# The order of four PSUM banks in the first slot of a feed-forward loop chunk

## The chip, the cores and the metric

The kernel runs on one core of a Trainium2 chip. The metric is the device time of one execution in microseconds (us), as the median of several runs; lower is better. The engines are called as the profile calls them: PE is TensorE (PEld its weight loads), DVE VectorE, ACT ScalarE, POOL GpSimd, and SP issues the weight transfers.

## What is computed

A stack of two transformer layers (an mLSTM mixer in the first, a differential attention in the second) with four feed-forward layers, two gated per-layer embeddings and a shared key-value projection, and behind it one hybrid block of convolution and dilated attention. 256 tokens, model width 1024, everything in float32. The change touches the four feed-forward layers alone, which are

```python
D_MODEL = 1024; SEQ = 256; D_FF = 2816

def rms_norm(x, g):
    xf = x.astype(jnp.float32)
    y = xf * lax.rsqrt(jnp.mean(xf * xf, axis=-1, keepdims=True) + EPS)
    return (y * g.astype(jnp.float32)).astype(x.dtype)

def swiglu(x, w_in, w_out):
    gate, up = jnp.split(x @ w_in, 2, axis=-1)
    return (jax.nn.silu(gate) * up) @ w_out
...
        h = swiglu(rms_norm(x, g[0]), w_ffn_in[layer, 0], w_ffn_out[layer, 0])
        x = x + 0.5 * rms_norm(h, g[1])
```

and the same again with g[4] and g[5], in both layers of the stack.

## The kernel before

**Weights come in slots.** All weights stream through one sequence of 226 slots of 128 x 2048 elements. SP loads a slot into one of three raw buffers, ACT rounds it to the format of the fast product (w_hi, L623), POOL subtracts to get the rest (w_lo, L590), and PE uses both. w_hi and w_lo have six buffers each. The activations are split in the same way (xT_hi, xT_lo), and a product is made of three: high by high, low weights by high activations, high weights by low activations.

**A feed-forward layer** has 11 chunks of 256 hidden columns. A chunk needs two slots for gate and up (four of the eight row blocks of the model width in each, "half" 0 and 1) and one slot for the down projection, which adds into the four acc banks. The layers are F0, F1, F2 and F3. Chunks 0, 1 and 10 are written out; chunks 2 to 9 are in a loop of four turns with two chunks in each (L2158), so there are 32 loop chunks in the whole kernel. The order in the loop is: gate and up of chunk n, down projection of chunk n-1, gate and up of chunk n+1, and so on.

**In a loop chunk** (`gate_up_rows`, L2052) the hidden columns are the rows of the result, so the weights are the stationary operand. Per row block k, per part (gate, up) and per half of the columns j there is a `high` product (L2067): w_hi against xT, whose 512 columns are the high and the low activations of 256 tokens, and a `low` product (L2073): w_lo against the 256 columns of xT_hi, added into the first half of the same bank. That is 16 high and 16 low products in a slot. Gate goes to the banks gu[:, 0] and tb[:, 1], up to gu[:, 1] and tb[:, 0]. A bank is opened by the high product of k = 0 of the first slot and closed in the second.

**What the banks wait for.** The gate banks of the chunk before must have been read (the wait for h_ready), and the up banks too: DVE multiplies up by the activated gate in place (L1326), ACT copies its high half out (L801) and DVE subtracts the low half (L1330), which counts ht_lo_ready. In the first loop chunk of a layer (n = 2) the hidden values of chunk 1 come by another way: PE turns them with four transposes into tb[:, 0] right ahead of the chunk (L2108), ACT copies the high half (L731, L767), and DVE subtracts the low half in one instruction (L1358 in F0 and F2, L1384 in F1 and F3), which counts ht_lo_ready.

**After a slot** the last products count tile0_used and slot_used, by which ACT knows that a buffer of w_hi may be written again; the last gate products of the second slot count gate_in_psum, on which DVE starts to scale the gate (L1312 to L1315).

Of the kernel before, what the change touches and what calls it, by code (L numbers as in the profile page):

```python
# [31 lines left out]
P = 128  # L32
# [5 lines left out]
NIT = FF // CH  # L38
# [98 lines left out]
def program(nc, A, out):  # L137
    ctx = ExitStack()
    with ctx:
        def sb(name, shape, dt=F32):  # L140
            return ctx.enter_context(nc.sbuf_tensor(name, shape, dt))

        def sem(name):
            return ctx.enter_context(nc.semaphore(name))
# [3 lines left out]
        w_hi = sb("w_hi", [P, NSPL, SLOT], F32R)  # L148
        w_lo = sb("w_lo", [P, NSPL, SLOT], F32R)
        xT = sb("xT", [P, KT, 2, TILES * P], F32R)  # L150
        xT_hi, xT_lo = xT[:, :, 0, :], xT[:, :, 1, :]
# [76 lines left out]
        at = 1024  # L228
# [48 lines left out]
        tile0_used = sem("tile0_used")  # L277
        slot_used = sem("slot_used")
# [11 lines left out]
        h_ready = sem("h_ready")  # L290
        ht_in_psum = sem("ht_in_psum")
        ht_hi_ready = sem("ht_hi_ready")
        ht_lo_ready = sem("ht_lo_ready")
        rs_row_in_psum = sem("rs_row_in_psum")
        rs_row_ready = sem("rs_row_ready")
        gate_in_psum = sem("gate_in_psum")
# [58 lines left out]
        def ht_count(f, n, t=0):  # L355

            return (NIT + 1) * f + n + 1 + t
# [1572 lines left out]
        def _(pe):  # L1930
            mm = nc.tensor.matmul
# [117 lines left out]
            def ffn(name, following):  # L2049
                f, s0 = FFN_NO[name], S[name]  # L2050

                def gate_up_rows(n, i, a):  # L2052

                    for half in range(2):
                        slot = a.plus(half)
                        pe.wait_ge(lo_ready, slot.count())
                        for part, pair_of in enumerate((gate_rows, up_rows)):
                            if half == 0 and part == 0:  # L2060
                                pe.wait_ge(h_ready, i * 4 + (2 * NIT * f + 2 * n))
                            if half == 0 and part == 1:
                                pe.wait_ge(ht_lo_ready, i * 2 + ht_count(f, n - 1))

                            def high(k, j):
                                at = 512 * k + 256 * part + P * j
                                return mm(pair_of(j), w_hi[:, slot.spl, at:at + P],  # L2067
                                          xT[:, 4 * half + k, :, :].rearrange("p a c -> p (a c)"),
                                          start=(half == 0 and k == 0), stop=(half == 1 and k == 3))

                            def low(k, j):
                                at = 512 * k + 256 * part + P * j
                                return mm(pair_of(j)[:, 0:2 * P], w_lo[:, slot.spl, at:at + P],  # L2073
                                          xT_hi[:, 4 * half + k, :], start=False, stop=False)

                            for k in range(4):
                                for product in ((high, low), (low, high))[half == 1 and k == 3]:
                                    done = [product(k, j) for j in range(2)]
                            for j in range(2):
                                if part == 1:  # L2080
                                    done[j].then_inc((tile0_used, slot_used)[j], 1)
                                elif half == 1:
                                    done[j].then_inc(gate_in_psum, 1)

                def down_n(n, turn, slot):

# [71 lines left out]
                with pe.Fori(0, (NIT - 3) // 2) as i:  # L2158
                    for d in (0, 1):
                        gate_up_rows(2 + d, i, At(s0 + 5 + 3 * d, i))  # L2160
                        down_n(1 + d, i, At(s0 + 7 + 3 * d, i))


                n, a = NIT - 1, At(s0 + FFN_SLOTS - 4)
# [514 lines left out]
```

## Time and profile before

| | |
|---|---|
| median of three runs | 1376.75 us (1374.72 to 1377.45) |
| the profiled execution | 1375.41 us, its span 1373.4 us |
| granted clock of PE, mean | 0.999 |
| PE busy | 1357.0 us, 99% of the span |
| POOL busy | 1134.7 us, 83% |
| ACT and DVE busy | 662.9 us and 606.5 us |
| loop chunks | 32, in four groups that start at 43.3, 339.2, 602.2 and 860.0 us |

Times in the rows below are microseconds from the start of the span. A row of the timeline has the start, the time that it covers, the engine and line, the operation with its output and inputs, how many instructions were merged into the row (x), and in square brackets the idle time of the engine just before it with what ended that. Matmuls overlap: one of 512 columns shows 0.39 us, but the next starts earlier than that, so the distance from start to start is what a product costs.

### The profile page before, as it was taken

How to read it: one execution, taken by the hardware profiler on the slowest of the kernel's cores; microseconds unless marked ns; L12 is line 12 of the kernel's file. 1: busy time of each engine (PE TensorE's matmuls, PEld its weight loads, DVE VectorE, ACT ScalarE, POOL GpSimd, SP SyncE). 2: the span in 40 equal slices, each digit the busy share in tenths (PEclk: the TensorE clock that was granted, in tenths of full speed). 3: DMA queues.
4: the chain of work that ended last, by engine and by line, in shares of the span. 5: the costliest groups of instructions: out<-in, count | busy, mean ns of one | idle time of the engine just before them, and what ended most of it. 6: DMA issues, size and time to landing. Idle time of an engine off the chain costs nothing.

```text
span 1373.4 us, 19730 instructions
## 1 busy us (share of the span) xinstructions
PE 1357.0 (99%) x6803; PEld 1127.9 (82%) x6803; DVE 606.5 (44%) x1554; ACT 662.9 (48%) x773; POOL 1134.7 (83%) x913
## 2 busy tenths in 40 slices
PE   8999999999999999999999999999999999999997
PEld 5888888888888888888888778888888888888886
DVE  6233344654333356323333885333356135762224
ACT  5444444556444455544443675444446444554531
POOL 5999977849999967999998549999968987679882
PEclk9999999999999999999999999999999999999999
DMA  8666654627655545666555426655545554346550
GB/s 271 214 204 205 203 184 142 203 85 230 203 194 184 192 160 180 214 191 207 183 183 186 138 81 206 214 187 183 185 163 189 186 182 154 128 153 240 184 170 31
DMA packets 160960, 246.98 MB, mean 180 GB/s; under 512 B 8924, under 2 KB 99844, under 8 KB 160772
## 3 DMA queue, kind: packets, MB, share of 16 engines
q1 hardware_dynamic: 158612, 239.42, 53.3%
q10 hardware_dynamic: 2288, 6.75, 1.3%
q8 instruction: 38, 0.62, 0.2%
q14 instruction: 22, 0.18, 0.0%
HBM read 245.10 MB, written 1.05 MB: 179 GB/s over the span
## 4 chain that ended last, share of the span: by engine, by line
POOL 59%; PE 21%; issue 17%; DMA 1%; ACT 0%; DVE 0%; POOLq 0%; SPq 0%; ACTq 0%; DVEq 0%
POOL w_lo L590 59%; PE acc L1981 5%; PE acc L1984 5%; PE acc L1982 5%; DMA w_raw<-in_w_ffn_in 1%; PE tb L1984 1%; PE tb L1982 1%; PE gu L1982 1%; PE tb L1981 1%; PE gu L1984 1%; PE gu L1981 1%; PE tb L2552 1%; PE gu L2517 0%; PE tb L2526 0%; DMA x_res<-in_x 0%
## 5 line engine op out<-in xcount | busy, mean ns | idle before, releaser
L590 POOL TENSOR_TENSOR w_lo<-w_raw,w_hi 128x512 fp32r<-128x512 f32 x896 | 1129.7, 1305 | 211.7 <-ACT w_hi L623 209.2
L623 ACT CAST w_hi<-w_raw 128x2048 fp32r<-128x2048 f32 x225 | 427.6, 1909 | 135.9 <-DMA w_raw<-in_w_ffn_in 37.0
L2067 PE MATMUL gu<-xT,w_hi 128*128 128x512 f32 x512 | 202.4, 395 | 0.0
L2067 PE MATMUL tb<-xT,w_hi 128*128 128x512 f32 x512 | 202.2, 395 | 0.0
L1981 PE MATMUL acc<-w_hi,xT 128*128 128x512 f32 x496 | 198.2, 400 | 0.0
L1982 PE MATMUL acc<-w_lo,xT 128*128 128x512 f32 x496 | 193.2, 389 | 0.0
L1984 PE MATMUL acc<-w_hi,xT 128*128 128x512 f32 x468 | 182.7, 390 | 0.0
L1312 DVE TENSOR_TENSOR arena<-gu,arena 128x256 f32<-128x256 f32 x64 | 27.2, 424 | 300.5 <-PE gu L2067 300.5
L2073 PE MATMUL tb<-xT,w_lo 128*128 128x256 f32 x512 | 140.3, 280 | 0.0
L2073 PE MATMUL gu<-xT,w_lo 128*128 128x256 f32 x512 | 139.8, 279 | 0.0
L1981 PE MATMUL gu<-w_hi,xT 128*128 128x512 f32 x312 | 123.7, 396 | 2.2 <-ACT xT L655 2.0
L1982 PE MATMUL gu<-w_lo,xT 128*128 128x512 f32 x312 | 121.5, 389 | 0.0
L2073 PEld LDWEIGHTS tb<-xT,w_lo 128*128 128x128 f32 x512 | 96.4, 188 | 20.2
L2073 PEld LDWEIGHTS gu<-xT,w_lo 128*128 128x128 f32 x512 | 96.2, 188 | 19.1
L1982 PEld LDWEIGHTS acc<-w_lo,xT 128*128 128x128 f32 x496 | 93.3, 188 | 18.2 <-issue 0.2
L1981 PEld LDWEIGHTS acc<-w_hi,xT 128*128 128x128 f32 x496 | 93.3, 188 | 18.3 <-issue 0.6
L1984 PEld LDWEIGHTS acc<-w_hi,xT 128*128 128x128 f32 x468 | 87.8, 188 | 18.8
L797 ACT ACTIVATE arena<-gu 128x256 f32<-128x256 f32 x32 | 12.3, 383 | 184.4 <-DVE gu L1315 184.3
L2067 PEld LDWEIGHTS tb<-xT,w_hi 128*128 128x128 f32 x512 | 97.1, 190 | 2.6
L2067 PEld LDWEIGHTS gu<-xT,w_hi 128*128 128x128 f32 x512 | 96.3, 188 | 2.5
L1984 PE MATMUL gu<-w_hi,xT 128*128 128x512 f32 x192 | 74.9, 390 | 0.0
L1981 PEld LDWEIGHTS gu<-w_hi,xT 128*128 128x128 f32 x312 | 58.6, 188 | 14.5 <-issue 2.5
(373 smaller groups left out, 2057.4 us busy)
## 6 DMA issues: line engine op xcount, KB each, us to landing
w_raw<-in_w_ffn_in SPq DMA_DIRECT2D x176, 512.0 KB, 4.6
w_raw<-in_w_ffn_out SPq DMA_DIRECT2D x88, 512.0 KB, 4.2
w_raw<-in_w_in SPq DMA_DIRECT2D x80, 512.0 KB, 4.5
w_raw<-in_mlstm_w_in SPq DMA_DIRECT2D x24, 512.0 KB, 4.3
w_raw<-in_w_ple_gate SPq DMA_DIRECT2D x16, 512.0 KB, 4.3
w_raw<-in_w_kv SPq DMA_DIRECT2D x16, 512.0 KB, 4.3
w_raw<-in_mlstm_w_out SPq DMA_DIRECT2D x8, 512.0 KB, 4.5
w_raw<-in_diff_w_q SPq DMA_DIRECT2D x8, 512.0 KB, 4.1
```

The source lines that it names most:

```text
L590: ins = pool.tensor_tensor(w_lo[:, slot.spl, cols], w_raw[:, slot.raw, cols], w_hi[:, slot.spl, cols].bitcast(F32), ALU.subtract)
L623: nc.scalar.copy(w_hi[:, slot.spl, :], w_raw[:, slot.raw, :]).then_inc(hi_ready, 1)
L797: nc.scalar.activation(sg[:, j, :], gate_rows(j)[:, 0:2 * P], ACT.Silu).then_inc(silu_ready, 1)
L1312: v.tensor_tensor(part, low, rs_row, ALU.mult).then_inc(row_step, 1)
L1981: mm(out, xh, wh, start=(half == 0 and k == 0), stop=False)
L1982: mm(out, xh, wl, start=False, stop=False)
L1984: last = mm(out, xl, wh, start=False, stop=(half == 1 and k == 3))
L2067: return mm(pair_of(j), w_hi[:, slot.spl, at:at + P], xT[:, 4 * half + k, :, :].rearrange("p a c -> p (a c)"), start=(half == 0 and k == 0 ...
L2073: return mm(pair_of(j)[:, 0:2 * P], w_lo[:, slot.spl, at:at + P], xT_hi[:, 4 * half + k, :], start=False, stop=False)
L2552: ins = nc.tensor.transpose(tb[:, 1, tok(k)], h_s[:, H_PLACE[c], t, tok(k)], ident[:])
```

## The change

In the first slot of a loop chunk the two loops over part and over k change places. Before, all 16 gate products ran through k = 0 to 3, high j = 0, 1 then low j = 0, 1, and then the 16 up products likewise. Now each k has four high products (gate, gate, up, up) and then four low ones in the same order of banks. The wait for ht_lo_ready, which stood ahead of the up products, stands now ahead of the first up product of k = 0, that is behind the second product of the slot. The slot's counts stay on its last two products. The second slot keeps its order.

```diff
--- before.py
+++ after.py
@@ -2056,31 +2056,35 @@
                     for half in range(2):
                         slot = a.plus(half)
                         pe.wait_ge(lo_ready, slot.count())
-                        for part, pair_of in enumerate((gate_rows, up_rows)):
-                            if half == 0 and part == 0:
-                                pe.wait_ge(h_ready, i * 4 + (2 * NIT * f + 2 * n))
-                            if half == 0 and part == 1:
-                                pe.wait_ge(ht_lo_ready, i * 2 + ht_count(f, n - 1))
-
-                            def high(k, j):
-                                at = 512 * k + 256 * part + P * j
-                                return mm(pair_of(j), w_hi[:, slot.spl, at:at + P],
-                                          xT[:, 4 * half + k, :, :].rearrange("p a c -> p (a c)"),
-                                          start=(half == 0 and k == 0), stop=(half == 1 and k == 3))
-
-                            def low(k, j):
-                                at = 512 * k + 256 * part + P * j
-                                return mm(pair_of(j)[:, 0:2 * P], w_lo[:, slot.spl, at:at + P],
-                                          xT_hi[:, 4 * half + k, :], start=False, stop=False)
-
+
+                        def high(k, part, j):
+                            at = 512 * k + 256 * part + P * j
+                            return mm((gate_rows, up_rows)[part](j), w_hi[:, slot.spl, at:at + P],
+                                      xT[:, 4 * half + k, :, :].rearrange("p a c -> p (a c)"),
+                                      start=(half == 0 and k == 0), stop=(half == 1 and k == 3))
+
+                        def low(k, part, j):
+                            at = 512 * k + 256 * part + P * j
+                            return mm((gate_rows, up_rows)[part](j)[:, 0:2 * P], w_lo[:, slot.spl, at:at + P],
+                                      xT_hi[:, 4 * half + k, :], start=False, stop=False)
+
+                        if half == 0:
+                            pe.wait_ge(h_ready, i * 4 + (2 * NIT * f + 2 * n))
                             for k in range(4):
-                                for product in ((high, low), (low, high))[half == 1 and k == 3]:
-                                    done = [product(k, j) for j in range(2)]
+                                for product in (high, low):
+                                    for part in range(2):
+                                        if k == 0 and part == 1 and product is high:
+                                            pe.wait_ge(ht_lo_ready, i * 2 + ht_count(f, n - 1))
+                                        done = [product(k, part, j) for j in range(2)]
                             for j in range(2):
-                                if part == 1:
-                                    done[j].then_inc((tile0_used, slot_used)[j], 1)
-                                elif half == 1:
-                                    done[j].then_inc(gate_in_psum, 1)
+                                done[j].then_inc((tile0_used, slot_used)[j], 1)
+                            continue
+                        for part in range(2):
+                            for k in range(4):
+                                for product in ((high, low), (low, high))[k == 3]:
+                                    done = [product(k, part, j) for j in range(2)]
+                            for j in range(2):
+                                done[j].then_inc((tile0_used, slot_used)[j] if part else gate_in_psum, 1)
 
                 def down_n(n, turn, slot):
 
```

## Rows read from the trace of the kernel before

**Rows 1.** The page: the span, busy times, and the granted clock in 40 slices.

```profile
span 1373.4 us, 19730 instructions
PE 1357.0 (99%) x6803; PEld 1127.9 (82%) x6803; DVE 606.5 (44%) x1554; ACT 662.9 (48%) x773; POOL 1134.7 (83%) x913
PEclk9999999999999999999999999999999999999999
```

**Rows 2.** Waits of PE over the span: us in total, times, longest.

```profile
PE gu L1981 <- ACT xT L655: 2.0, 1, 2.0
...
PE gu L1981 <- POOL w_lo L590: 0.2, 1, 0.2
```

**Rows 3.** The page's groups of instructions: high products of the loops on gu.

```profile
L2067 PE MATMUL gu<-xT,w_hi 128*128 128x512 f32 x512 | 202.4, 395 | 0.0
```

**Rows 4.** Timeline of PE: first and twelfth of twelve products on one bank.

```profile
303.64 0.39 PE L1981 MATMUL acc<-w_hi,xT 128*128 128x512 f32 x1
...
306.14 0.39 PE L1984 MATMUL acc<-w_hi,xT 128*128 128x512 f32 x1
```

**Rows 5.** Timeline of PE: a down projection, 24 products, and the chunk behind it.

```profile
54.58 0.62 PE L2016 MATMUL acc<-w_hi,hT_hi 128*128 128x512 f32 x2
...
60.03 0.39 PE L2067 MATMUL gu<-xT,w_hi 128*128 128x512 f32 x1
```

**Rows 6.** Timeline of PE, steady chunk: gate k=0 and k=2, up, second slot, down, next.

```profile
126.66 0.39 PE L2067 MATMUL gu<-xT,w_hi 128*128 128x512 f32 x1
...
128.04 0.40 PE L2067 MATMUL gu<-xT,w_hi 128*128 128x512 f32 x1
...
129.43 0.40 PE L2067 MATMUL gu<-xT,w_hi 128*128 128x512 f32 x1
...
132.22 0.40 PE L2067 MATMUL gu<-xT,w_hi 128*128 128x512 f32 x1
...
137.82 0.62 PE L2016 MATMUL acc<-w_hi,hE_hi 128*128 128x512 f32 x2
...
143.28 0.39 PE L2067 MATMUL gu<-xT,w_hi 128*128 128x512 f32 x1
```

**Rows 7.** Timeline, first loop chunk of F0: products one and three, DVE's low half.

```profile
43.34 0.48 PE L2067 MATMUL gu<-xT,w_hi 128*128 128x512 f32 x1
...
43.89 0.28 PE L2073 MATMUL gu<-xT,w_lo 128*128 128x256 f32 x1
...
44.24 0.69 DVE L1358 TENSOR_TENSOR hT_lo<-tb,hT_hi 128x512 fp32r<-128x512 f32 x1 [1.88 <-ACT hT_hi L731]
```

**Rows 8.** Timeline: third chunk of F0, its low half, and that of the sixth.

```profile
76.80 0.39 PE L2067 MATMUL gu<-xT,w_hi 128*128 128x512 f32 x1
...
77.35 0.41 DVE L1330 TENSOR_TENSOR hT_lo<-tb,hT_hi 128x256 fp32r<-128x256 f32 x1
...
125.08 0.42 DVE L1330 TENSOR_TENSOR hE_lo<-tb,hE_hi 128x256 fp32r<-128x256 f32 x1
```

**Rows 9.** Timeline, first loop chunk of F1: first product, DVE's low half.

```profile
339.16 0.48 PE L2067 MATMUL gu<-xT,w_hi 128*128 128x512 f32 x1
...
340.06 0.69 DVE L1384 TENSOR_TENSOR hT_lo<-tb,hT_hi 128x512 fp32r<-128x512 f32 x1 [5.34 <-ACT hT_hi L767]
```

**Rows 10.** Timeline, second loop chunk of F0: ACT, DVE, products 17 and 18.

```profile
59.83 1.91 ACT L623 CAST w_hi<-w_raw 128x2048 fp32r<-128x2048 f32 x1 [2.80 <-DMA w_raw<-in_w_ffn_in]
...
62.38 0.41 DVE L1330 TENSOR_TENSOR hE_lo<-tb,hE_hi 128x256 fp32r<-128x256 f32 x1
...
62.84 0.50 PE L2067 MATMUL gu<-xT,w_hi 128*128 128x512 f32 x1
63.18 0.39 PE L2067 MATMUL tb<-xT,w_hi 128*128 128x512 f32 x1
```

**Rows 11.** Timeline: POOL's back-to-back stretch in F0; ACT ahead of the third chunk.

```profile
46.66 30.10 POOL L590 TENSOR_TENSOR w_lo<-w_raw,w_hi 128x512 fp32r<-128x512 f32 x24
...
74.80 1.91 ACT L623 CAST w_hi<-w_raw 128x2048 fp32r<-128x2048 f32 x1 [2.87 <-DMA w_raw<-in_w_ffn_in]
```

## Prediction

> **What bounds the kernel now.** I read the page's busy times first, then the waits of TensorE, then the rows of the two loop chunks in order of time. TensorE (PE) is busy for 99% of the span, GpSimd (POOL) for 83% [rows 1]. The chain that ended last runs mostly through POOL, so I looked at what PE really waited for: in the whole span the matmul line L1981 waited 2.0 us once for ScalarE and 0.2 us once for POOL, and no wait of PE is longer [rows 2]. PE never runs short of split weights; it is the bound, and the chain is drawn through POOL only because POOL works back to back in the same time. What adds time to PE's stream therefore adds it to the span, unless a later wait of PE shrinks by the same amount, and there is hardly a later wait that could.
>
> The edit touches the first of the two slots of each gate-and-up chunk. There are 32 such chunks: eight in each of four feed-forward layers. A slot is 16 products of 512 columns ("high") and 16 of 256 columns ("low"), so the loops hold 512 high products on gu and on tb each [rows 3], and half of them lie in first slots.
>
> **Part 1, what is removed or added: nothing.** The same 32 products, with the same operands, lengths and weight loads, stand in a first slot before and after. The increments of the slot stay on its last two products, and the second slot is the same. DMAs, POOL's, ACT's and DVE's instructions stay as they are. Only two things move: the order of banks, and the wait for ht_lo_ready.
>
> **Part 2, the order of banks (spacing of products).** First, does it matter to a product which bank the one before it wrote? Eleven products in a row on one bank of acc go from 303.64 to 306.14, 2.50 / 11 = 0.227 us each [rows 4]. In the down projections two banks alternate, and 24 products take from 54.58 to 60.03, 5.45 / 24 = 0.227 us each [rows 5]. So one bank or two is the same to 0.001 us, and I expect no more from four.
>
> What does cost is the mix of lengths. At 0.227 us for 512 columns and half of that, 0.1135 us, for 256, a slot would take 16 x 0.3405 = 5.45 us. A chunk in the steady state takes 132.22 - 126.66 = 5.56 us for the first slot and 137.82 - 132.22 = 5.60 us for the second [rows 6]. So 0.11 us of a first slot is excess. If four banks removed it all, the gain would be 0.11 x 32 = 3.5 us, or 4.0 us with the rounding of the rows against me (0.125 us a chunk): the bound of a gain.
>
> The other bound comes from the second slot. It has two places at which four low products stand in a row (the low ones of k=2, then k=3 begins with its own low ones), one in the gate part, with four high ones behind it, and one in the up part; the first slot has no such place. It takes 0.04 us more, and the first slot has a cheap first group: its first two k-steps take 1.38 us, the next two 1.39 and the four of the up part 2.79 [rows 6]. Set aside the cheap entrance of 0.01 us, and two runs of four lows cost 0.03 us of the 0.04: about 0.015 us each, 0.02 at most. The changed first slot has four runs of "four high, four low" in place of eight of "two, two". The first keeps its cheap entrance from the down products; the three others cost 0.015 us each: 0.045 us a chunk, x 32 = 1.4 us slower. Bounds of this term: 4.0 us faster and 0.02 x 4 x 32 = 2.6 us slower. I take +1.4, since the rows with a run of four lows are of the very products that are moved.
>
> The Trainium skill (Perfetto Trace Analysis, section Matmul Optimizations) says that all eight PSUM banks should be put to use so that more can go on at once. By that rule the four banks would be worth something, up to the 4.0 us above; by the rows of one bank and of two they are worth nothing.
>
> **Part 3, the wait for ht_lo_ready moves up by 14 products.** Now PE passes it behind 16 gate products, some 2.78 us into the chunk; after the change behind two, 0.45 us into it (0.54 us where a transpose stands ahead: 43.89 - 43.34 [rows 7]). Behind the wait stands all of PE's stream, and behind that the gate and up results for which DVE and ACT wait. What matters is when VectorE has written the last of the low halves of h, which is what the semaphore counts.
>
> In the steady state it is in time. Before the chunk that starts at 126.66 the last subtraction ends at 125.08 + 0.42 = 125.50 [rows 8], 1.16 us ahead of the start. Twenty-five of the 32 chunks repeat these rows to 0.01 us, and one has its low half 0.45 us ahead; they cost nothing, and the cover has 1.16 + 0.45 = 1.6 us left. The wait for h_ready stays at the chunk's start; it counts an earlier step of the same chain on DVE and was never seen to bind.
>
> It is late in the first chunk of each layer. There the low half is made from transposes that PE issues just ahead of the chunk, then a copy on ACT, then one subtraction on DVE. In layer F0 the chunk starts at 43.34, the third product at 43.89, and DVE ends at 44.24 + 0.69 = 44.93 [rows 7]. In F1 the chunk starts at 339.16 and DVE ends at 340.06 + 0.69 = 340.75 [rows 9]: 1.59 us into the chunk in both, and the other two layers repeat it. What PE needs to restart I read at the one place where this very wait already binds, in the second chunk of F0: DVE ends at 62.38 + 0.41 = 62.79, and the product behind the wait starts at 62.84, 0.05 us later; its successor follows after 0.34 us in place of 0.23, so another 0.10 us goes into filling up again [rows 10]. The stall of a first chunk is then 1.59 + 0.05 - 0.54 + 0.10 = 1.20 us, and four of them are 4.8 us.
>
> The second chunk of F0 is the fifth place. It starts at 60.03 [rows 5] and the low half is ready at 62.79; it now loses 0.14 us (0.04 ahead of the product at 62.84 and 0.10 behind it). Its time is not set by PE: ACT's copies of h stand behind a 1.91 us weight cast at 59.83 that waited for a DMA, while POOL subtracts back to back from 46.66 to 76.76 [rows 10, 11]. So it stays at 62.79 when PE comes later. PE comes 1.20 us later, reaches its third product at 60.03 + 1.20 + 0.45 = 61.68, and starts it at 62.84: 1.16 + 0.10 = 1.26 us of stall, less the 0.14 that goes, +1.12 us net. The third chunk of F0 starts at 76.80 now and at 79.1 then [rows 8]; its low half is ready at 77.35 + 0.41 = 77.76 [rows 8], again behind a cast that waited for a DMA [rows 11], so it is in time by then. Sum of part 3: 4.80 + 1.12 = 5.9 us. Its bounds are narrow, 5.5 us without the refill of 0.10 in four of the five places, and 6.6 us if the low half of F0's third chunk moved with PE, so that this chunk had to wait too (77.76 + 0.05 - 77.25 + 0.10 = 0.66).
>
> The skill has a rule that speaks against this change (Perfetto Trace Analysis, section Matmuls): groups should rotate through banks so that the emptying of one overlaps with the products of the next. Taking all four banks at once gives that overlap up for a slot: the up banks used to be emptied under 16 gate products.
>
> **How the numbers follow.** +5.9 (stalls) + 1.4 (spacing) = +7.3 us on the profiled run. That run took 1375.41 us, of which 1373.4 are its span; the median of the three runs is 1376.75, 1.3 us above it, and I add the sum to the median: 1376.75 + 7.3 = 1384.1 us, +0.53%. About 0.2% (2.75 us) is what a measurement of this kernel can tell from no change.
>
> **Rivals.** (a) *Rotation pays.* The excess of the mixed slots is the reuse of a bank two products later, and goes: 1376.75 + 5.9 - 4.0 = 1378.7 us, within 0.2%. Against it: one bank in a row shows no such cost. Chance 6%. (b) *The stalls are given back.* PE's stalls sit in five places, and with PE later, POOL and the DMAs are further ahead, so later waits shrink. That would leave 1.4 us or so: 1378 us. Against it: PE's listed waits of 2.0 and 0.2 us are at 14 us or too small to give back 5.9. Chance 4%. (c) *Faster.* If four banks in turn let the array take one column in every cycle of the granted 2.4 GHz (the granted clock is 0.9 or more in every slice [rows 1]), a first slot would take 16 x (512 + 256) / 2.4 = 5.12 us, an estimate, in place of 5.56: 0.44 x 32 = 14.1 us won, 1376.75 + 5.9 - 14.1 = 1368.6 us. It decides from 5.9 / 32 = 0.18 us won per chunk. For it speaks that 0.227 us is more than 512 / 2.4 = 0.213; against it that one bank and two give the same 0.227, so the rest isn't a matter of banks. Chance 3%. On this the skill (TensorE: Matmul & The Clock Gate, section Back-to-back issue gap) gives 512 columns 215.7 ns when nothing else binds; by that the slot would be 5.2 us, close to (c), but the trace shows 0.227 us throughout. (d) *The change stalls steadily*: if the wait were late in every chunk, not in five, 32 x 1.2 = 38 us, 1415 us. The rows at 125.50 exclude it by 1.6 us; 1%. The forecast has 86%.
>
> Range: spacing from 0 to +2.6 and stalls from 5.5 to 6.6 give 1382.3 to 1386.0; the median of runs can sit 1 us to either side; reaching a little towards (a), where part of the excess goes, the range is 1380.8 to 1386.8. Chances: slower by over 0.2% 0.87 (the forecast and (d)), within 0.2% 0.10 ((a) and (b)), faster 0.03 ((c)).
>
> **What would show it.** In the changed trace: in the first chunk of each layer a gap of about 1.2 us behind the second product, ended by the DVE subtraction L1358 or L1384; in the second chunk of F0 one of 1.26 us ended by L1330 at about 62.8; no gap in the others. The period of a steady loop chunk with its down projection, now 143.28 - 126.66 = 16.62 us [rows 6], should be 16.64 to 16.68. If it is 16.50 or less, rival (a) or (c) holds and the spacing term is wrong in sign. If the first-chunk gaps are there but the span is not longer, (b) holds.

## The result, and the profile after

| | before | after |
|---|---|---|
| median of the runs | 1376.75 us (5 runs) | 1382.63 us (5 runs, 1381.60 to 1384.39) |
| ratio | | 1.0051, 95% interval 1.0040 to 1.0061 |
| span of the profiled execution | 1373.4 us | 1379.7 us |
| granted clock of PE, mean | 0.999 | 0.999 |

The kernel became slower, by 5.9 us in the medians and by 6.3 us in the two profiled spans. The quotient of the two medians is 1.0043; it lies inside the interval of the recorded ratio, which in microseconds reaches from 5.5 to 8.4. So the total alone fixes the size of the change only to about 3 us, and the steps below are read from the traces. The page of the changed kernel shows the same count of instructions as [rows 1] and hardly another busy time. The groups of instructions show where the wait went: the high products on gu (L2062, formerly L2067, [rows 3]) now have idle time ahead of them.

```profile
span 1379.7 us, 19730 instructions
PE 1359.2 (99%) x6803; PEld 1128.9 (82%) x6803; DVE 608.1 (44%) x1554; ACT 662.8 (48%) x773; POOL 1134.3 (82%) x913
...
L2062 PE MATMUL gu<-xT,w_hi 128*128 128x512 f32 x512 | 202.6, 396 | 5.2 <-DVE hT_lo L1384 1.9
```

The waits of PE, in us in total, times and longest, answer [rows 2]. Three lines are new, and they are the five places that the prediction named: two first chunks with L1384 (F1, F3), two with L1358 (F0, F2), and one chunk with L1330.

```profile
PE gu L2062 <- DVE hT_lo L1384: 1.9, 2, 0.9
PE gu L2062 <- DVE hT_lo L1358: 1.8, 2, 0.9
PE gu L1981 <- ACT xT L655: 1.7, 1, 1.7
PE gu L2062 <- DVE hE_lo L1330: 1.5, 1, 1.5
```

The timeline of the first loop chunk of F1, against [rows 9]: two products go, then nothing until DVE's subtraction ends at 342.74 + 0.69 = 343.43, and the third starts at 343.49. The wait view calls that 0.94 us, because it takes a matmul of 0.40 us as busy to its end; from start to start it is 343.49 - 342.15 = 1.34 us where 0.23 would do, and about 0.1 us more is lost behind the third (its successor starts 0.33 us later, not 0.23).

```profile
341.84 0.48 PE L2062 MATMUL gu<-xT,w_hi 128*128 128x512 f32 x1
342.15 0.40 PE L2062 MATMUL tb<-xT,w_hi 128*128 128x512 f32 x1
...
342.74 0.69 DVE L1384 TENSOR_TENSOR hT_lo<-tb,hT_hi 128x512 fp32r<-128x512 f32 x1 [5.34 <-ACT hT_hi L767]
...
343.49 0.50 PE L2062 MATMUL gu<-xT,w_hi 128*128 128x512 f32 x1 [0.94 <-DVE hT_lo L1384]
```

The second loop chunk of F0, against [rows 10]. The third product starts at 63.15, 1.68 us after the 61.47 at which it would have followed. ACT's cast, which began at 59.83 in the kernel before, begins here at 60.14, when its DMA has landed; the copies behind it and the subtraction are later by as much.

```profile
60.14 1.91 ACT L623 CAST w_hi<-w_raw 128x2048 fp32r<-128x2048 f32 x1 [2.55 <-DMA w_raw<-in_w_ffn_in]
...
61.01 0.39 PE L2062 MATMUL gu<-xT,w_hi 128*128 128x512 f32 x1
61.24 0.39 PE L2062 MATMUL tb<-xT,w_hi 128*128 128x512 f32 x1
...
62.68 0.41 DVE L1330 TENSOR_TENSOR hE_lo<-tb,hE_hi 128x256 fp32r<-128x256 f32 x1
...
63.15 0.50 PE L2062 MATMUL gu<-xT,w_hi 128*128 128x512 f32 x1 [1.52 <-DVE hE_lo L1330]
63.49 0.39 PE L2062 MATMUL tb<-xT,w_hi 128*128 128x512 f32 x1
```

A steady chunk, against [rows 6]: first slot from 129.31 to 134.90, second to 140.49, next chunk at 145.94. The low half of the chunk before (127.73 + 0.42 = 128.15) is 1.16 us ahead of the start, as in [rows 8].

```profile
127.73 0.42 DVE L1330 TENSOR_TENSOR hE_lo<-tb,hE_hi 128x256 fp32r<-128x256 f32 x1
...
129.31 0.39 PE L2062 MATMUL gu<-xT,w_hi 128*128 128x512 f32 x1
...
134.90 0.40 PE L2062 MATMUL gu<-xT,w_hi 128*128 128x512 f32 x1
...
140.49 0.39 PE L2016 MATMUL acc<-w_hi,hE_hi 128*128 128x512 f32 x1
...
145.94 0.39 PE L2062 MATMUL gu<-xT,w_hi 128*128 128x512 f32 x1
```

The two slots take 5.59 and 5.59 us where they took 5.56 and 5.60: the first lost 0.024 us and the second, whose order was not touched, won 0.017. Over six steady chunks of F1 (second to eighth) the difference can be read without rounding trouble: 455.61 - 355.89 = 99.72 us before and 459.52 - 359.76 = 99.76 after, that is 0.007 us a chunk and 0.2 us in all 32. First the two rows of the kernel before, then those of the changed one:

```profile
355.89 0.39 PE L2067 MATMUL gu<-xT,w_hi 128*128 128x512 f32 x1
...
455.61 0.39 PE L2067 MATMUL gu<-xT,w_hi 128*128 128x512 f32 x1
```

```profile
359.76 0.39 PE L2062 MATMUL gu<-xT,w_hi 128*128 128x512 f32 x1
...
459.52 0.39 PE L2062 MATMUL gu<-xT,w_hi 128*128 128x512 f32 x1
```

For all kernels below, the table has the stretch from the first product of a layer's first loop chunk to that of its eighth, in us, taken from the starts in the traces. It leaves out everything ahead of the loops, which differs from run to run (last section).

| kernel | F0 | F1 | F2 | F3 | sum |
|---|---|---|---|---|---|
| before | 116.55 | 116.45 | 116.43 | 116.43 | 465.86 |
| after | 119.43 | 117.69 | 117.66 | 117.66 | 472.44 |
| e1_wait_only | 118.42 | 117.62 | 117.62 | 117.61 | 471.27 |
| e2_early_turn | 116.41 | 116.39 | 116.39 | 116.39 | 465.58 |
| e3_runs_of_four | 116.45 | 116.51 | 116.45 | 116.45 | 465.86 |
| e4_four_banks_by_twos | 116.34 | 116.34 | 116.34 | 116.34 | 465.36 |
| e5_wait_behind_eight | 118.19 | 116.67 | 116.68 | 116.71 | 468.25 |
| e9_early_turn_f1_f3 | 118.93 | 116.39 | 116.39 | 116.39 | 468.10 |
| e10_copies_before_cast | 117.69 | 116.39 | 116.39 | 116.39 | 466.86 |
| e11_wait_at_front | 118.31 | 116.45 | 116.42 | 116.47 | 467.65 |
| e12_old_order_both_fixes | 116.41 | 116.34 | 116.34 | 116.34 | 465.43 |

The change added 6.6 us to the loops and 6.3 us to the span. Of the 0.3 us between them, 0.2 lie ahead of F0's loop, where nothing was changed yet (it starts at 43.13 and not at 43.34); the stretches between the loops and behind the last are shorter by 0.1 us in all.

### The profile page after: what moved, and what is told of

Same layout as the page of the kernel before. It is cut to its first block, busy times and chain, and to the rows that moved or that the text cites. A ratio compares the mean times of both kernels' runs of the same rounds, so it can differ in the third digit from the quotient of the medians.

```text
span 1379.7 us, 19730 instructions
## 1 busy us (share of the span) xinstructions
PE 1359.2 (99%) x6803; PEld 1128.9 (82%) x6803; DVE 608.1 (44%) x1554; ACT 662.8 (48%) x773; POOL 1134.3 (82%) x913
## 3 DMA queue, kind: packets, MB, share of 16 engines
HBM read 245.10 MB, written 1.05 MB: 178 GB/s over the span
## 4 chain that ended last, share of the span: by engine, by line
POOL 58%; PE 21%; issue 18%; DMA 1%; DVE 1%; ACT 1%; POOLq 0%; SPq 0%; ACTq 0%; DVEq 0%
POOL w_lo L590 58%; PE acc L1981 5%; PE acc L1984 5%; PE acc L1982 5%; PE tb L1984 1%; PE tb L1981 1%; PE tb L1982 1%; PE gu L1981 1%; PE gu L1982 1%; PE gu L1984 1%; PE tb L2556 1%; PE gu L2521 0%; PE tb L2530 0%; DMA w_raw<-in_w_ffn_in 0%; ACT w_hi L623 0%
## 5 line engine op out<-in xcount | busy, mean ns | idle before, releaser
L2062 PE MATMUL gu<-xT,w_hi 128*128 128x512 f32 x512 | 202.6, 396 | 5.2 <-DVE hT_lo L1384 1.9
L2062 PE MATMUL tb<-xT,w_hi 128*128 128x512 f32 x512 | 201.6, 394 | 0.0
L2068 PE MATMUL tb<-xT,w_lo 128*128 128x256 f32 x512 | 135.2, 280 | 0.0
L2068 PE MATMUL gu<-xT,w_lo 128*128 128x256 f32 x512 | 134.5, 280 | 0.0
L2062 PEld LDWEIGHTS gu<-xT,w_hi 128*128 128x128 f32 x512 | 96.5, 188 | 15.2 <-DVE hT_lo L1384 2.7
L2062 PEld LDWEIGHTS tb<-xT,w_hi 128*128 128x128 f32 x512 | 96.9, 189 | 7.9
```

What stands on the lines that cost most here:

```text
L2062: return mm((gate_rows, up_rows)[part](j), w_hi[:, slot.spl, at:at + P], xT[:, 4 * half + k, :, :].rearrange("p a c -> p (a c)"), start=(h ...
L2068: return mm((gate_rows, up_rows)[part](j)[:, 0:2 * P], w_lo[:, slot.spl, at:at + P], xT_hi[:, 4 * half + k, :], start=False, stop=False)
```

## The experiments

The theory is that the wait, moved up by 14 products, makes nearly all of the loss. The rival is that the order of four banks costs something by itself, in each chunk.

### The wait alone, and the order alone

e1 keeps the old order and moves only the wait:

```diff
-                            if half == 0 and part == 1:
-                                pe.wait_ge(ht_lo_ready, i * 2 + ht_count(f, n - 1))
...
                                     done = [product(k, j) for j in range(2)]
+                                    if half == 0 and part == 0 and k == 0 and product is high:
+                                        pe.wait_ge(ht_lo_ready, i * 2 + ht_count(f, n - 1))
```

> The kernel before with one edit: the wait for ht_lo_ready stands behind the first two gate products, the order of products is the old one. Theory (the moved wait carries the change): gaps of about 1.2 us behind the second product in the first loop chunk of each layer and one of 1.5 to 2.0 us in the second chunk of F0, none elsewhere; steady period 16.62 us as before; span +6.0 to +6.6 us, as long as that of the changed kernel to within 0.5 us. Rival (the order of the banks is what costs): no more than 1 us slower than before.

Measured: 1381.88 us, ratio to before 1.0042 (1.0028 to 1.0056), where the whole change had 1.0051 (1.0040 to 1.0061). (The profiled execution was 7.0 us longer in its span than that of the kernel before; 1.5 of these lie ahead of F0's loop, as the last section tells.) The loops of F1 to F3 are 1.17 to 1.19 us longer than before, the changed kernel's 1.23 to 1.24. The waits are the same ones:

```profile
PE gu L2070 <- DVE hT_lo L1358: 1.9, 2, 0.9
PE gu L2070 <- DVE hT_lo L1384: 1.9, 2, 0.9
```

The gap in F0's second chunk was 0.81 us, not the 1.5 to 2.0 expected; more on that below. In three layers the wait alone gives the change's loss to 0.07 us, most of which is the 0.007 us a chunk. The rival is out as a large cost.

e3 has the other half: two banks and the old wait, but runs of four high and four low products in the first slot.

```diff
-                            for k in range(4):
+                            if half == 0:
+                                for k2 in (0, 2):
+                                    for product in (high, low):
+                                        for k in (k2, k2 + 1):
+                                            done = [product(k, j) for j in range(2)]
+                            for k in range(4) if half else ():
```

> The kernel before with one edit: in each half of the first slot (gate, then up, two banks each) the products run four high, four low, as in the changed kernel, and the wait stays behind 16 gate products. If the mix of lengths causes the 7 ns by which a steady chunk grew (11.168 to 11.175 us): period 16.627 us, no gaps, span +0.2 us. If four banks cause it: period 16.620 us.

e4 turns it round: four banks, but lengths by twos, on top of e2 (below).

```diff
                             for k in range(4):
-                                for product in (high, low):
-                                    for part in range(2):
+                                for part in range(2):
...
+                                    for product in (high, low):
```

> As the early-turn kernel, but each k of the first slot runs gate high, gate low, up high, up low (two and two), so the four banks are taken in turns of two and the lengths alternate as before the change. If lengths cause the 7 ns: period 16.620 us; if the banks do: 16.627 us. The wait stands behind four products in place of two, so the gap in F0's second chunk is 0.2 us shorter than in the early-turn kernel.

The timeline of PE in F1, from the second to the eighth chunk, first for e3 and then for e4:

```profile
357.64 0.39 PE L2067 MATMUL gu<-xT,w_hi 128*128 128x512 f32 x1
...
457.40 0.39 PE L2067 MATMUL gu<-xT,w_hi 128*128 128x512 f32 x1
```

```profile
359.07 0.39 PE L2062 MATMUL gu<-xT,w_hi 128*128 128x512 f32 x1
...
458.79 0.39 PE L2062 MATMUL gu<-xT,w_hi 128*128 128x512 f32 x1
```

99.76 us with two banks and runs of four, as in the changed kernel; 99.72 us with four banks and runs of two, as before. So the 0.007 us a chunk belong to the order of lengths, and taking four banks in place of two costs and wins nothing. The starts within one steady chunk say the same: from product to product e3 and the changed kernel agree to about 1 ns, and so do e4 and the kernel before. F0's second chunk had no gap at all in e4 (its loop is 116.34 us), so what was expected of that gap could not be read. Each ran once, in 1377.36 and 1378.76 us. e3's span of 1375.3 us is 1.9 us over the kernel before, and 1.8 of these lie ahead of F0's loop, not in the loops; e4's loop in F0 begins 3.4 us late, in part for the reason given at e2.

### Taking away what makes the wait late

In a first chunk the low half is late because PE turns chunk 1's hidden values right ahead of the loop. e2 turns them one tile of a down projection earlier, in all four layers; so that nothing is overwritten, chunk 0's halves go to hE.

```diff
-                    hi, lo = h_rows(n) if n else (hT_hi, hT_lo)
+                    hi, lo = h_rows(n)
                     for t in range(TILES):
                         down_tile(slot, hi, lo, t, n == 0, False)
+                        if t == 0 and between:
+                            between()
...
-                down_n(0, None, At(s0 + 4))
-                turn_h(1, hs_next if name in SKEWED else hs)
+                down_n(0, None, At(s0 + 4), lambda: turn_h(1, hs_next if name in SKEWED else hs))
```

and L731, L767, L1358 and L1384 write h_rows(n) in place of hT.

> The changed kernel with the cause of the first-chunk waits taken away: chunk 0's hidden halves go to the other pair of buffers (hE), and the transposes of chunk 1's hidden values stand between the two tiles of the down projection ahead of the loop, 2.7 us earlier. Theory: the four first-chunk gaps of 1.2 us are gone (4.8 us), the gap in the second chunk of F0 stays and grows to about 2.4 us since PE comes 1.2 us earlier to it while its low half is ready at the same time; span 1375.9 to 1376.5 us, 3.3 to 3.8 us under the changed kernel. Rival (order of banks): still about 6 us over the kernel before.

Measured: 1379.15 us, 1.0020 (1.0011 to 1.0029) of before. All four first-chunk gaps are gone, and each loop takes 116.4 us. But the total is 3.3 us over before and not 2.5 to 3.1, and it is made of something else: the gap in F0's second chunk, expected to grow to 2.4 us, was not there, and a new loss appeared ahead of F0's loop, which began at 48.42 in place of 43.34. By then the low half of the second chunk was in time (ready at 63.91, the chunk at 65.07). Ahead of F0's loop DVE has chunk 1's hidden values too late for the earlier transposes, PE waits 1.92 us, and the products behind run at about half speed, 0.99 us for two in place of 0.45. The granted clock was 0.50 (the lower level, 1.2 GHz) from 44 to 47 us. In e4 PE waited 1.59 us at the same place and the granted clock stayed at 1.00; what decides between the two is not shown. The profiled execution of e2 was the slowest of its kernel (1380.45 us), so its other executions need not have this stretch. First the timeline of PE, then the view by windows (the stretch, busy PE, PEld, DVE, ACT and POOL with their counts, granted clock, DMA share, GB/s):

```profile
43.56 0.99 PE L2114 MATMUL tb<-ident,arena 128*128 128x128 f32 x4 [1.92 <-DVE arena L1339]
44.21 1.20 PE L2016 MATMUL acc<-w_hi,hE_hi 128*128 128x512 f32 x2
45.20 1.05 PE L2019 MATMUL acc<-w_lo,hE_hi 128*128 128x512 f32 x2
```

```profile
44.00:45.00 1.00, 1.00 (x5) 0.90 (x4) 0.00 (x0) 0.41 (x1) 1.00 (x2) 0.50 0.41 143
```

So e9 leaves F0 as it was:

```diff
+                down_n(0, None, At(s0 + 4),
+                       None if name == "F0" else lambda: turn_h(1, hs_next if name in SKEWED else hs))
+                if name == "F0":
+                    turn_h(1)
```

> The changed kernel with the transposes of chunk 1's hidden values between the two tiles of the down projection, and chunk 0's hidden halves in hE, in F1, F2 and F3 only; F0 keeps its place for them. Theory: the loops of F1, F2 and F3 take 116.4 us each in place of 117.7 (3.8 us in all), F0's loop stays at 118.4 to 119.4; 3.5 to 3.8 us under the changed kernel, 2.2 to 3.2 over the kernel before; and F0's prelude, which the early turn lengthened by some 3 us, is back. Rival (the early turn costs elsewhere what it saves): the stretches between the loops grow by 1 us each.

Measured: 1378.21 us, 1.0018 (1.0009 to 1.0027). That is 2.4 us over the kernel before, where 2.2 to 3.2 were expected, and 4.4 us under the changed kernel, more than the 3.5 to 3.8 expected: F0's loop too was 0.5 us shorter, by a smaller gap in its second chunk. The loops of F1, F2 and F3 take 116.39 us, and the stretches between them are 0.01 to 0.14 us longer, not 1 us. In F1 the subtraction now ends at 339.33 + 0.69 = 340.02, 1.24 us ahead of the chunk:

```profile
339.33 0.69 DVE L1384 TENSOR_TENSOR hT_lo<-tb,hT_hi 128x512 fp32r<-128x512 f32 x1 [2.62 <-ACT hT_hi L767]
...
341.26 0.39 PE L2062 MATMUL gu<-xT,w_hi 128*128 128x512 f32 x1
341.49 0.39 PE L2062 MATMUL tb<-xT,w_hi 128*128 128x512 f32 x1
341.72 0.39 PE L2062 MATMUL gu<-xT,w_hi 128*128 128x512 f32 x1
```

### The size of the stall

If a stall is (low half) minus (time of the products ahead of the wait), it can be dosed. e5 puts eight products ahead of the wait, e11 none.

```diff
-                            for k in range(4):
-                                for product in (high, low):
-                                    for part in range(2):
-                                        if k == 0 and part == 1 and product is high:
...
+                            for k2 in (0, 2):
+                                for part in range(2):
+                                    if k2 == 0 and part == 1:
+                                        pe.wait_ge(ht_lo_ready, i * 2 + ht_count(f, n - 1))
+                                    for k in (k2, k2 + 1):
+                                        for product in (high, low):
```

> The changed kernel with blocks of two k: eight gate products, then eight up products, twice, so that the wait for ht_lo_ready stands behind eight products (1.48 us into a first chunk) in place of two. Theory (stall = time from the chunk's start to the low half, 1.59 + 0.05, less the time of the products ahead of the wait, + 0.10 to fill up): 0.26 us in each first chunk, so F1, F2 and F3 loops are 116.7 us each (116.4 without a stall, 117.7 in the changed kernel), and the whole is within 2 us of the kernel before. Rival (a cost per chunk of opening all four banks early, whenever the wait is met): loops as long as in the changed kernel.

Measured: 1378.16 us, 1.0016 (1.0006 to 1.0025), 2.4 us over before, a little outside the 2 us. F1 to F3 take 116.67, 116.68 and 116.71 us: 0.22 to 0.28 us over before where 0.26 was worked out. F0's second chunk stalled 1.5 us all the same (1.4 more than in the kernel before), and that is the rest. e11 is the kernel before with the wait moved to the front:

```diff
                                 pe.wait_ge(h_ready, i * 4 + (2 * NIT * f + 2 * n))
-                            if half == 0 and part == 1:
                                 pe.wait_ge(ht_lo_ready, i * 2 + ht_count(f, n - 1))
```

> The kernel before, order of products untouched, with the wait for ht_lo_ready ahead of the first product of the chunk. Theory: the first-chunk stall is 1.59 + 0.05 and what it takes to fill up, so 1.65 to 1.8 us in place of 1.2; the loops of F1, F2 and F3 take 118.0 to 118.3 us each; F0's second chunk stalls 0.45 us more than with the wait behind two products. Steady chunks still none (cover 1.16 us): period 16.620 us.

Measured in one execution: 1384.24 us. The view of waits, below, has each first-chunk wait 0.5 us longer than in the changed kernel, and in the timeline behind it the first product of F1's loop starts 0.06 us after DVE ends (343.75 + 0.69 = 344.44):

```profile
PE gu L2065 <- DVE hT_lo L1384: 2.8, 2, 1.4
PE gu L2065 <- DVE hT_lo L1358: 2.8, 2, 1.4
```

```profile
343.75 0.69 DVE L1384 TENSOR_TENSOR hT_lo<-tb,hT_hi 128x512 fp32r<-128x512 f32 x1 [5.34 <-ACT hT_hi L767]
...
344.50 0.50 PE L2065 MATMUL gu<-xT,w_hi 128*128 128x512 f32 x1 [1.40 <-DVE hT_lo L1384]
```

The expectation put these stalls into the loops; standing ahead of the first product, they lie in the stretch before it, which grew from 179.27 to 180.91 us ahead of F1, by 1.64 us, and by 1.56 and 1.66 us ahead of F2 and F3. That is 1.59 + 0.05 with nothing to fill up again, because the product behind the transposes pays that anyway. So the stalls are 1.6, 1.2 and 0.26 us behind 0, 2 and 8 products, as worked out from the one row each. What was expected of F0's second chunk, 0.45 us more than with the wait behind two products, did not come: it stalled 1.8 us, as in the changed kernel.

### F0's second chunk

e10 is e9 with ScalarE's two copies of h ahead of its third weight cast in each loop chunk:

```diff
-                    ahead(a.plus(2))
                     for j in range(2):
                         act.wait_ge(h_ready, i * 4 + (2 * NIT * f + 2 * n + j + 1))
                         nc.scalar.copy(h_rows(n)[0][:, j, :], up_rows(j)[:, 0:2 * P]).then_inc(row_hi_ready, 1)
+                    ahead(a.plus(2))
```

> As the early turn in F1 to F3, and in every loop chunk ScalarE copies the high halves of h out of the up banks before its third weight cast, not behind it. Theory (F0's second chunk waits because the copies stand behind a cast that waits for its DMA): the gap in F0's second chunk goes, F0's loop is 116.4 + 1.2 = 117.6 us, the other three 116.4; 0.5 to 1.9 us under the run with the early turn alone, about 1.2 us over the kernel before. Rival (the late low half in F0 comes from DVE or PE): the gap stays.

Measured: 1377.52 us, 1.0011 (1.0002 to 1.0021), 0.7 us under e9. F0's loop takes 117.69 us, 1.3 more than the others by its first chunk; the second has no gap. The copy of the second bank is made at 60.76, as soon as DVE has written it, and the cast follows:

```profile
60.76 0.38 ACT L800 CAST hE_hi<-tb 128x256 fp32r<-128x256 f32 x1 [1.31 <-DVE tb L1326]
61.03 1.92 ACT L623 CAST w_hi<-w_raw 128x2048 fp32r<-128x2048 f32 x1
...
61.17 0.42 DVE L1330 TENSOR_TENSOR hE_lo<-tb,hE_hi 128x256 fp32r<-128x256 f32 x1
...
62.74 0.39 PE L2062 MATMUL gu<-xT,w_hi 128*128 128x512 f32 x1
```

The low half is ready at 61.59, 1.15 us ahead of the chunk, as in the steady state. So it was the place behind the cast that made this one late. That this execution began its loop late is not the reason: e1's began at the same 44.8 and had the gap. In the kernels with the old place the low half was ready 1.05 us after the end of the cast (in e2 1.35), and the cast began when its DMA had landed, at 59.83 in the kernel before, 60.14 in the changed one and 59.46 in e9.

Last, e12 has both edits on the kernel before, with its order and wait untouched:

> The kernel before, order of products and place of the wait untouched, with the two edits that took waits away: the early turn in F1 to F3 and ScalarE's copies ahead of its third cast. If it could beat the kernel before, it would be by what waits there still cost: 0.09 us at each of three loop entries (a transpose stands no longer just ahead) and 0.14 us in F0's second chunk. Loops of 116.34 us in F1 to F3 (116.43 to 116.45 before) and 116.4 in F0 (116.55), 0.1 us back in each stretch ahead of a loop: no difference that can be measured, within 0.1% of before.

Measured: 1376.0 us, 1.0004 (0.9995 to 1.0013), and loops shorter by 0.43 us in all. Its total cannot be told from the kernel before, so no kernel here is shown to beat that. In F0's second chunk the low half is now ready at 60.04, 2.75 us earlier than before, which is e10's finding once more.

## Why the prediction was right

The forecast was 1384.1 us in a range of 1380.8 to 1386.8; measured were 1382.63. The mechanism held: five stalls at the moved wait, in the five chunks named. Two sizes did not, and their errors partly cancelled. By its steps:

- **PE is the bound, so a stall goes through to the end.** Right. 6.6 us more in the loops became 6.3 us of span. Rival (b), stalls given back later, was 0.1 us.
- **The steady state is covered.** Right: 27 chunks show no gap, and in all of them the low half is 1.15 to 1.16 us ahead. F0's third chunk is among them, as forecast, though not at the time worked out: its low half was ready at 78.28, not at 77.76, and the chunk began at 79.43.
- **First chunks, 1.20 us each.** Right: from the first chunks' lengths the stalls are 1.19, 1.20, 1.19 and 1.19 us. e5 and e11 show that the formula behind it holds at other places of the wait.
- **F0's second chunk, +1.12 us net.** Mechanism right, size off: 1.65 us net (12.97 us for its products where they took 11.32; 1.79 over a steady chunk). The step that failed is "so it stays at 62.79 when PE comes later": it was ready at 63.09, 0.30 us later, as the cast ahead of the copies began 0.31 us later; and PE came 0.21 us earlier than worked out, since F0's loop began at 43.13 and not at 43.34. Over a steady chunk the gap was 0.81 us in e1, 1.27 in e9, 1.5 in e5 and 1.8 in e11 (there ahead of the chunk), and in e2 and e4 there was none. e9 has the changed kernel's order and wait in F0, and still its cast began 0.68 us earlier, though its loop began only 0.17 us earlier. So this time varies by more than the error, and one profile doesn't fix it; what makes the transfer land earlier or later was not tried.
- **Spacing, +1.4 us.** Wrong in size: +0.2 us, 0.007 a chunk, and a period of 16.63 us where 16.64 to 16.68 had been forecast. The working took the second slot's 0.04 us as the price of its two runs of four low products. But with the first slot changed, the untouched second slot became 0.017 us faster: part of its excess hung on what ran ahead of it. e3 and e4 give the 0.007 us to the lengths and nothing to the banks. Nor is a 512-column product 0.227 us everywhere, as the last words on rival (c) have it: in the mixed slots its successor follows after 0.22 to 0.24 us, before and after the change.
- **Rival (a) and (c), rotation pays.** Out: e4 has four banks and the very period of before, 99.72 us for six chunks.

The two errors of size, +0.5 and -1.2 us, go in opposite directions; with them the sum of part 2 and part 3 would have been 6.6 us, where the forecast added 7.3. That the total came within 1.5 us owes something to this and to the spread of the medians.

## What to carry to other kernels

Where one engine is 99% busy, what matters of a reordering is what it puts behind a wait: take each wait that moves, and compare the time of its release with the time at which the engine gets to it, at the loop's entry and while the pipeline still fills as well as in the steady state. In the changed kernel 27 of 32 chunks had 1.6 us in hand, and five cost all but 0.2 us of the loss. F0's third, 2.6 us later than in the kernel before, is among the 27; in that kernel its low half came 0.96 us into the chunk, under the cover of the 16 gate products, so it was not safe to begin with. To take more banks earlier in a chunk gives up the time in which they used to be emptied; that is free only if something else covers it.

## What the hardware showed that was not expected

**Accumulating products don't care which bank came before.** One bank in a row, two in turn and four in turn all give 0.226 to 0.227 us for 512 columns (the four are the first high products of a changed slot, 129.31 to 130.22). The order of lengths does matter, by little: runs of four and four cost 0.007 us a chunk of 64 products more than runs of two and two.

**The start-up varies, apart from the change.** F0's loop began at 43.0 to 43.5 us in before, after, e5, e9 and e12, and at 44.8 to 45.2 in e1, e3 and e10, none of which moves an instruction ahead of that loop (e11, at 45.27, has its own stall of 1.64 us there; e2 and e4 have the early turn in F0). In e1 the granted clock was 0.85 between 10 and 20 us of the span, where the kernel before has 1.00 (view by windows, before and then e1):

```profile
10.00:20.00 10.00, 7.42 (x33) 5.62 (x34) 7.43 (x19) 7.26 (x9) 3.68 (x3) 1.00 0.96 292
```

```profile
10.00:20.00 10.00, 7.42 (x27) 5.49 (x28) 7.39 (x19) 7.21 (x9) 3.71 (x4) 0.85 0.97 290
```

With the same 7.42 us of busy time PE got through 33 matmuls in the first and 27 in the second. e3 and e10 have 0.89 and 0.84 there; after, e9, e11 and e12 have 1.00. So the late starts go with a lower clock in that stretch. But e5 has a lower clock too and was not late:

```profile
10.00:20.00 10.00, 8.82 (x33) 6.61 (x34) 6.97 (x17) 6.74 (x7) 3.96 (x4) 0.83 0.97 290
```

There PE was busy for 8.82 us of the ten and got its 33 matmuls through. So a lower clock by itself does not make a late start, and what lowers it was not tried. This is why spans are compared by their loops here: 1.5 us of luck is more than one of the stalls in a first chunk.
